# Ten conditioning chunks of a four-layer kernel: from the second layer's recurrence to three feed-forwards

## What is computed

```python
for l in range(DEPTH):
    mod = silu_c @ w_ada[l] + b_ada[l]                       # 1024 -> 6 * 1024
    sh_a, sc_a, g_a, sh_f, sc_f, g_f = jnp.split(mod[:, None, :], 6, axis=-1)
    mc = jnp.split(silu_cc @ w_ada[l][:, :n_c] + b_ada[l][:n_c], n_c // d)   # the same for the context
    hx = rmsnorm(x) * (1 + sc_a) + sh_a
    ...
    rx, rc = hgrn_group(ux, uc, base_c, lb_all[:, l], hg_norm[l], ctx_out)   # the recurrence
    x = x + g_a * (jnp.concatenate([fx, ax, rx], axis=-1) @ w_out[l])
    x = x + g_f * swiglu(rmsnorm(x) * (1 + sc_f) + sh_f, w_gate[l], w_up[l], w_down[l])
```

## Time and profile before

| | us |
|---|---|
| median of 3 runs | 1833.6 (1831.87, 1833.6, 1841.55) |
| the profiled execution, its own time | 1837.19 |
| its span, first to last instruction | 1835.3 |
| TensorE busy | 1711.7 (93%) |
| VectorE busy | 1268.2 (69%) |
| ScalarE busy | 838.1 (46%) |
| mean granted TensorE clock | 0.967 |

### The profile page before, as it was taken

How to read it: one execution, slowest core, us unless ns; L and a number is a source line. 1 busy time by engine, 2 the same in 40 slices (tenths; PEclk the granted TensorE clock), 3 DMA queues, 4 the chain that set the end, 5 groups by cost and what they waited for, 6 DMA issues and landing times.

```text
span 1835.3 us, 25024 instructions
## 1 busy us (share of the span) xinstructions
PE 1711.7 (93%) x9438; PEld 1399.0 (76%) x9438; DVE 1268.2 (69%) x2218; ACT 838.1 (46%) x1626; POOL 84.3 (5%) x154
## 2 busy tenths in 40 slices
PE   4999888999999999999798999988899999979998
PEld 3778777798888888877677888776688877768886
DVE  1445977569998777478675788768577865767554
ACT  2523864343322332445644544457544545754442
POOL 1001042000000000001030000000000000000000
PEclk9899999999999999999788999999999999989999
DMA  9532022146577665243434877542497755246553
GB/s 300 191 115 77 22 93 70 54 131 188 184 235 230 211 205 168 81 140 98 138 94 132 279 265 268 197 134 50 144 291 242 241 194 162 70 138 211 179 170 128
DMA packets 270967, 299.19 MB, mean 163 GB/s; under 512 B 7984, under 2 KB 224800, under 8 KB 270720
## 3 DMA queue, kind: packets, MB, share of 16 engines
q1 hardware_dynamic: 269424, 293.44, 50.1%
q0 software_dynamic: 1424, 4.16, 1.0%
HBM read 296.52 MB, written 1.05 MB: 162 GB/s over the span
## 4 chain that ended last, share of the span: by engine, by line
PE 81%; DVE 8%; DMA 4%; ACT 4%; issue 3%; SPq 0%; DVEq 0%; ACTq 0%
PE bank L1163 78%; PE bank L1177 3%; DMA AWH<-in_w_ada 1%; DMA raw<-in_ffn_w_in 1%; DVE A L2989 1%; ACT whigh L1890 1%; DVE wlow L2534 1%; ACT A L2197 1%; DMA raw<-in_w_up 1%; DMA raw<-in_w_in 1%; DVE nmax L2962 0%; DVE SPARE L2551 0%; DVE PTA L2996 0%; DMA AWH<-in_ada_w 0%; DVE bank L3191 0%
## 5 line engine op out<-in xcount | busy, mean ns | idle before, releaser
L2534 DVE TENSOR_TENSOR wlow<-raw,whigh 128x2048 fp32r<-128x2048 f32 (+2 forms) x183 | 409.8, 2243 | 267.2 <-ACT whigh L1890 267.0
L1890 ACT ACTIVATE whigh<-raw 128x2048 fp32r<-128x2048 f32 (+2 forms) x183 | 344.4, 1882 | 349.4 <-PE bank L1163 167.7
L1163 PE MATMUL bank<-whigh,HTH 128*128 128x512 f32 (+1 forms) x1088 | 428.1, 394 | 22.8 <-issue 6.3
L1163 PE MATMUL bank<-whigh,HTL 128*128 128x512 f32 (+1 forms) x1088 | 418.7, 385 | 0.0
L1163 PE MATMUL bank<-wlow,HTH 128*128 128x512 f32 (+1 forms) x1088 | 418.6, 385 | 0.0
L1163 PEld LDWEIGHTS bank<-whigh,HTH 128*128 128x128 f32 x1088 | 208.2, 191 | 67.0 <-issue 27.4
L1163 PEld LDWEIGHTS bank<-whigh,HTL 128*128 128x128 f32 x1088 | 207.9, 191 | 41.0
L1163 PEld LDWEIGHTS bank<-wlow,HTH 128*128 128x128 f32 x1088 | 208.5, 192 | 38.4 <-issue 0.7
L1163 PE MATMUL bank<-whigh,hidden_high 128*128 128x512 f32 x440 | 173.7, 395 | 1.6 <-DVE wlow L2534 1.6
L1163 PE MATMUL bank<-whigh,hidden_low 128*128 128x512 f32 x440 | 171.5, 390 | 0.0
L1163 PE MATMUL bank<-wlow,hidden_high 128*128 128x512 f32 x440 | 171.3, 389 | 0.0
(11 more groups left out here) (263 smaller groups left out, 2193.9 us busy)
## 6 DMA issues: line engine op xcount, KB each, us to landing
raw<-in_ffn_w_in SPq DMA_DIRECT2D x88, 512.0 KB, 5.0
A<-in_ada_w SPq DMA_DIRECT2D x38, 1024.0 KB, 6.6
A<-in_w_ada SPq DMA_DIRECT2D x28, 1024.0 KB, 6.7
raw<-in_w_gate SPq DMA_DIRECT2D x44, 512.0 KB, 5.7
raw<-in_w_up SPq DMA_DIRECT2D x44, 512.0 KB, 7.9
raw<-in_ffn_w_out SPq DMA_DIRECT2D x20, 1024.0 KB, 5.1
raw<-in_w_down SPq DMA_DIRECT2D x18, 1024.0 KB, 6.7
raw<-in_w_in SPq DMA_DIRECT2D x14, 1024.0 KB, 6.1
```

Source lines behind the costliest of these rows:

```text
L1163: return nc.tensor.matmul(out, lhsT, rhs, start=start, stop=stop, skip_group_check=True)
L1890: nc.scalar.activation(parts(loads[n])[0], raw_slot(loads[n]), ACT.Copy).then_inc(*made("split_high", loads[n]))
L2534: V.tensor_tensor(low, raw_slot(loads[n]), as_float(high), ALU.subtract).then_inc(*made("split_low", loads[n]))
```

## The change

The ten chunks `(2, 8)` to `(2, 17)` leave the recurrence of layer 1. The first feed-forward gets 42 chunks where it had 36, the second 16 for 14, the third 14 for 12, and since chunks are dealt out in order, the later ones move forward too. With them go their loads in SP's queue and their slots in `AWH` and `U`. What TensorE did for them, VectorE does (`ada_sum`), in two more batches in the first and one more in the third feed-forward.

ScalarE gets a wait at the end of the recurrence of layer 1, until VectorE has weighed the last level of the last step. Before, it waited there for the sums of the last chunk, which TensorE formed behind the scores of that step.

```diff
@@ ada_plan @@
     give([("win", 0, *win_loads(0)[n]) for n in (0, 1, 2, 3, 3)] + scan(0, 7))
-    give(feed_forward(0, 36))
-    give(scan(1, 10))
-    give(feed_forward(1, 14))
-    give(feed_forward(2, 12))
+    give(feed_forward(0, 42))
+    give(feed_forward(1, 16))
+    give(feed_forward(2, 14))
     give(feed_forward(3, 4))
     return out
@@ recurrence(l), ScalarE @@
                 modulation_end()
                 if l == 0:
                     head_seeds(l, 2, 8)
+                else:
+                    act.wait_ge(*upto("weighed", l, steps[-1][0], LEVEL_ORDER[-1]))
```

## The result

The changed kernel takes **1855.5 us** (median of 4 runs, 1851.3 to 1861.6) against 1833.7 (1831.9 to 1841.6) on the same chip: a ratio of 1.0113, 95% interval 1.0081 to 1.0144. It is slower by 21.7 us. Run again beside the experiments it took 1849.4 against 1836.1, ratio 1.0065 [1.0045, 1.0086]; the two intervals just touch. So the loss is between 13 and 22 us; the forecast was 1838 (8 in 10 for 1828 to 1847), 4.2 above before. The profiled execution has a span of 1859.8 us (before 1835.3).

The account below looks back on a forecast made before the run. TensorE was taken to bound the feed-forwards, VectorE next, with no engine full in the second layer's recurrence. Recurrence -5, first part +9, later parts +0.2 gave +4.2 us: 1838 us, 8 in 10 for 1828 to 1847.

Parts of the forecast that it names:

- The recurrence (-5): Second layer's recurrence without its ten chunks: 5 us shorter, bounds -22 and +3.
- The chain of steps 0 to 3: Second layer's recurrence, from decay to decay on VectorE: 5.6 us gained without chunks between them.
- The small gains at the end: Second layer's recurrence: 1.2 us from ScalarE coming late once, 1.5 from a last small product before the output part.
- one fall more, worth 2 us: Second layer's recurrence: without chunks to fill TensorE, its clock drops once more to the lower level, costing 2 us.
- The signs that I named for this case: Second layer's recurrence: score matmuls of 6.24 us in steps 4 and 5 would show the forecast wrong.
- The rival with the clock: Lower clock in recurrence steps 4 and 5 takes the gain back, first feed-forward costs 9 to 12: 1845 us, chance 0.21.
- The first part (+9): First feed-forward with six more chunks: 9 us longer, bounds +2 and +25; growth under 4 or over 14 meant wrong.
- VectorE's backlog: First feed-forward: weight splits queue behind places with two chunks, making TensorE 6.5 us late in all by the second down load.
- Second and third part (+0.2): Second and third feed-forward, with two more chunks each: together 0.2 us longer, bounds -2 and +5.
- The stall near 1176: Second feed-forward: TensorE's 1.58 us wait for a split goes as a chunk moves away, -1.6 us.
- the +0.5 and the +0.4: Second part: +0.5 us for two chunks sharing a pair of loads at three places; third part: +0.4 for two chunks.
- The page weighed: VectorE's 256-wide multiply-add: row 0.484 us, skill 0.33; by the skill two chunks fit a place and 6.5 us vanish.

Follow-up runs that it names:

- The filled kernel: Changed kernel plus eight useless matmuls ending each of steps 4 to 7 of the second layer's recurrence; 1.0010 of the kernel before, recurrence 76.3 us.
- the shorter sums: Changed kernel; at first-part places 0, 2, 4 and 6 the second chunk does only 2 of 8 row blocks on VectorE; 1.0025 of the kernel before.
- The short transfers: Changed kernel; each chunk of the second and third part fetches one eighth of its bytes, with the same instructions; 1.0071 of the kernel before.

## Why the prediction was wrong

**The recurrence (-5): the size of the clock's term failed, and the gain is nothing.** The chain of steps 0 to 3 was right: 5.6 forecast, 5.4 to 6.5 measured. The small gains at the end (1.2 and 1.5) are not found. Against it stood "one fall more, worth 2 us", a fall being one of the clock from its upper level to the lower. That is the step that failed. A fall costs 6 to 7 us at the end alone: from step 7's decay to the first output matmul it is 25.7 to 27.4 us where the last scores take 3.34, and 31.9 to 33.9 where they take 6.24. The one profile of before that I had already contained this fall, so I took it for the rule there. With chunks in steps 4 to 6 it is chance: the last scores take longer than 3.34 us in four profiles of nine, and in one of the three with the old plan. With nothing in these gaps they take 6.24 in each of six, and part of the preparation of steps 6 and 7 is at the lower clock as well. Means of before (three profiles) and after (five with nothing in the recurrence) are 85.3 and 85.1 us: what the chain gains the clock takes.

The filled kernel shows that it is the clock: it adds work, and nothing else of a chunk, and its recurrence is 9 us shorter. That is one profile, but the ten executions behind 1.0010 against the seven behind 1.0065 point the same way for the whole kernel (some 10 us, of which the profiles at hand have 4 in the three feed-forwards). The signs that I named for this case (6.24 in steps 4 and 5) did not come: of the scores, only those of the last step are slow. The rival with the clock had the right mechanism, and with the slower preparation part of its price, but put the slow scores at the wrong steps.

The rule that I had weighed as that rival (Trainium skill, TensorE: Matmul & The Clock Gate, the section on oscillation: idle gaps between bursts send the array back to the lower clock) is borne out by the stretches here: 0.50 in the last without work in the gaps, 1.00 with it. Work in the gaps is no guarantee, as the 0.50 of the kernel before shows. That each step would begin low, as I read it, is borne out in part: the preparation of steps 6 and 7 begins or ends at the lower clock, but the scores of steps 4 to 6 take 3.34 us.

**The first part (+9): right queue, two terms missing.** It grew by 14.4 and 14.3 us in the two profiles (12.8 in three of the four others with the same places), within the bounds of +2 to +25 but above the 14 I had set as wrong. The idle time was 6.9 us (forecast 6.5 for VectorE's backlog), in another form: the second down load was not late by its split, but tile 10 by a drain. The drains of banks stand in the same queue as the splits, and I followed only the splits: that is the first missing term. The second is the clock, which was put at 0.7 and took 4.3: I had argued from a stretch whose idle time was broken up that a whole stall of 3 us would be harmless. The two batches took 2.6 in place of 1.8. These make 13.8; about half a microsecond has no place. That SP's queue costs nothing held: the shorter sums took all of the rest away with the transfers as they were.

**Second and third part (+0.2): the size failed.** They grew by 3.1 and 2.7 us in the first profile, 0.8 to 2.3 and 1.5 in the second (against 195.3 to 196.8 and 196.9). By the means of all profiles it is 1.3 and 1.8, together 3 in place of 0.2, within the bounds of -2 and +5. The stall near 1176 did go, but stalls of 0.9, 0.9 and 1.2 us came in the second part. The terms that failed are the +0.5 and the +0.4 for the moved chunks. I had costed them by VectorE's time alone and said nothing of their bytes here, though ScalarE already waited 65.6 us for weights in the second part and the rate there is 264 to 274 GB/s in the gate and up loads. The short transfers take 68 of 80 us of these waits away; whether they take the growth away is open in the second part, and in the third they do not.

**The added wait (0)** was right as far as can be seen: 1.0002 [0.9981, 1.0023] alone, and no sign of it in ScalarE's rows.

**The page weighed.** By the estimate of 0.33 us from the Trainium skill (VectorE: DVE Perf Modes, the section on the errata of SBUF sources) a double place would fit and the first part would not stall. (The same section of the Trainium skill says that this line of its table comes out too low for a measured copy.) The first part stalled; in the rows of after 14 multiply-adds take 6.30 us (478.20 to 484.50), 0.45 each, and the queue added up from the rows of before met the splits to 0.1 us. The measurement decides.

**The sum** by what is shown: +13 to +14.4 for the first part, 0 for the recurrence, +3 for the later ones (+6 in the first profile), 16 to 20 us. The two comparisons of medians give 13 and 22.

## What to carry to other kernels

Work that stands in the gaps of a latency-bound loop may be what keeps TensorE at its upper clock; moving it out has to be priced by what the loop costs at the lower level, over several profiles, since one profile holds one outcome of a chance. When an in-order engine gets more to do, follow everything in its queue that others wait for, drains and sums as well as the obvious product, and look at the longest single place and not the mean. And where a stage already waits for transfers, ask for the bytes of what is moved in, not only for its instructions; that they cost time here was not shown.

## What the hardware showed that was not expected

- Unchanged code has several outcomes: behind the first layer's recurrence the output began between 329.0 and 339.1 us, with the last scores at 3.59 us in most profiles, 6.24 in four and 5.68 and 5.91 in one each. The same changed kernel gave 6.24 and 3.60.
- Added work made a stage shorter: four times 3.64 us of useless matmuls took the recurrence from 85 to 76.3 us, four times 1.48 us to 79.5, in one profile each.
- Behind 3.7 us of idle time in the first part the 512-wide matmuls went at 0.43 us apart for some 5 us; after one of 2.75 us the first ones went at 0.23, and the next eight at 0.39 to 0.43. The cost of a stall here was its length and 2 us more.
